# A mixture-of-experts step on one Trainium2 core: expert steps of two kinds alternate, and the weights of an expert are acknowledged in two parts

## The reference, cut to what matters

```python
score = jax.nn.sigmoid(jnp.dot(h, p['w_router']))
_, idx = lax.top_k(score + p['router_bias'], TOP_K)          # TOP_K = 8, N_EXPERTS = 64
g = jnp.take_along_axis(score, idx, axis=-1)
g = ROUTE_SCALE * g / jnp.sum(g, axis=-1, keepdims=True)
# for every block of tokens of one expert e, with their gates gb:
a = jax.nn.silu(xb @ w_gate_e[e]) * (xb @ w_up_e[e])
yb = a @ w_down_e[e]
acc = acc.at[tb].add(yb * gb[:, None])
shared = (jax.nn.silu(h @ p['w_gate_s']) * (h @ p['w_up_s'])) @ p['w_down_s']
```

## Time and profile before

| | us |
|---|---|
| median of three runs | 1594.47 |
| profiled execution, its own time | 1584.53 |
| profiled execution, span from first to last instruction | 1582.8 |
| TensorE busy | 1394.0 (88%) |
| VectorE busy | 650.3 (41%) |
| mean granted TensorE clock | 0.942 of full speed |

### The profile page before, as it was taken

The page is one execution under the profiler, slowest core; times in us unless marked ns, Lnnn a source line. Parts: engine busy times, 40 slices in busy tenths (PEclk is TensorE's granted clock), DMA queues, the critical chain, the costliest instruction groups (busy, mean ns, idle before and its releaser), DMA issues. The chain is left out here.

```text
span 1582.8 us, 30737 instructions
## 1 busy us (share of the span) xinstructions
PE 1394.0 (88%) x10030; PEld 741.6 (47%) x10031; DVE 650.3 (41%) x1888; ACT 387.5 (24%) x1026; POOL 245.3 (15%) x287
## 2 busy tenths in 40 slices
PE   6999799999989999788878877677999989999992
PEld 3445566666667776434543322222333333444441
DVE  1423266776676766244552222121222222332333
ACT  1102255444544444320100111111111111111110
POOL 1000200005263320010000111111121211122120
PEclk9999799999999999989799988888999999999996
DMA  8312499998989999760066999999999999975835
GB/s 306 58 27 63 153 297 291 326 319 288 304 276 300 320 305 317 254 239 27 21 249 233 368 374 380 374 369 375 365 371 355 370 368 364 350 234 182 273 80 196
DMA packets 159517, 424.12 MB, mean 268 GB/s; under 512 B 47825, under 2 KB 49906, under 8 KB 133234
## 3 DMA queue, kind: packets, MB, share of 16 engines
q1 hardware_dynamic: 142912, 381.59, 66.6%
q0 software_dynamic: 14400, 38.82, 10.0%
q10 hardware_dynamic: 2098, 2.35, 0.5%
HBM read 395.25 MB, written 41.06 MB: 276 GB/s over the span
## 5 line engine op out<-in xcount | busy, mean ns | idle before, releaser
L2475 PE MATMUL ps_gu<-ring,mixT 128*32 128x512 f32 (+2 forms) x1664 | 362.4, 633 | 68.5 <-SPq L2233 67.6
L2475 PEld LDWEIGHTS ps_gu<-ring,mixT 128*32 128x32 f32 (+2 forms) x1664 | 125.0, 140 | 301.7 <-issue 251.4
L2494 PE MATMUL ps_y<-w_dn,aT_e 128*32 128x512 f32 (+2 forms) x832 | 175.9, 598 | 4.5 <-DVE aT_e L2389 1.9
L1427 PE MATMUL ps_kT<-ident,ring 128*128 128x128 f32 x1024 | 144.5, 284 | 15.9 <-DVE ring L1093 8.5
L1427 PEld LDWEIGHTS ps_kT<-ident,ring 128*128 128x128 f32 x1024 | 116.3, 146 | 75.3 <-issue 48.6
L2387 DVE TENSOR_TENSOR act_in<-sil,ps_gu 128x256 f32<-128x256 f32 x48 | 20.2, 421 | 301.8 <-ACT sil L2307 301.8
L2259 POOL DMA_INDIRECT kT<-h_dram,idx x50 | 51.9, 1037 | 587.1 <-DVE idx L2348 587.1
L2307 ACT ACTIVATE sil<-ps_gu 128x256 f32<-128x256 f32 x48 | 18.4, 383 | 408.1 <-PE ps_gu L2475 408.1
L1093 DVE COPY ring<-ps_kT 128x512 f32<-128x512 f32 x128 | 87.8, 686 | 39.4 <-PE ps_kT L1427 38.4
L2263 POOL DMA_INDIRECT sums_dram<-qT,sidx x48 | 76.5, 1593 | 147.9 <-DVE qT L2397 143.9
L2494 PEld LDWEIGHTS ps_y<-w_dn,aT_e 128*32 128x32 f32 (+2 forms) x832 | 55.4, 132 | 93.4 <-issue 85.7
(11 more groups left out here) (504 smaller groups left out, 1796.0 us busy)
## 6 DMA issues: line engine op xcount, KB each, us to landing
ring<-in_cache_k SPq DMA_DIRECT2D x256, 256.0 KB
ring<-in_cache_v SPq DMA_DIRECT2D x256, 256.0 KB, 4.6
ring<-in_w_gate_e SPq DMA_DIRECT2D x64, 1024.0 KB
ring<-in_w_up_e SPq DMA_DIRECT2D x64, 1024.0 KB
w_dn<-in_w_down_e SPq DMA_DIRECT2D x64, 1024.0 KB
w_in<-in_w_in SPq DMA_DIRECT2D x8, 1028.0 KB, 16.3
sums_dram<-w_dn SPq DMA_DIRECT2D x1, 4608.0 KB, 19.6
ring<-in_w_out SPq DMA_DIRECT2D x1, 4096.0 KB, 13.0
```

What stands on the lines that cost most here:

```text
L1427: last = pe.transpose(ps_kT[:, j % 2, e * PAGE:(e + 1) * PAGE], k_places[n % RING][:, e * DA + j * P:e * DA + (j + 1) * P], m.ident[:, :])
L2475: last = pe.matmul(ps_gu[at, :].rearrange("p (g n) -> p g n", g=2), xgT[:, u, k, at], w_gu[:, place, :, k, :].rearrange("p s g n -> p (s g ...
L2494: last = pe.matmul(ps_y[at, n, :], aT[:, j, at], w_dn[:, place, j, n * 512:(n + 1) * 512].rearrange("p s n -> p (s n)"), start=(j == 0), s ...
```

## The change

The steps get a new order. With S2 steps of class two and S4 of class four (rounded up to even), the first A = min(S2, S4) - 2 steps of each kind alternate: a step of class two at each even place, one of class four at each odd place. Then come the other steps of class four, then the other steps of class two, then those of class three, as three loops on TensorE (`n_mix`, `n_four`, `n_two`) instead of two. The loads follow that order: before the two experts of a class-two step comes the expert of the class-four step of the same pair, if that step begins a new expert. In the alternating part a class-two step uses slots 0 and 1, and the experts of class four use slots 2 and 3 in turn; the slot of a load is now read from a table, `slot_tab`, as well. That needs more table work: the ranks, the step of each lane and the slots are computed on GpSimd in 51 instructions with 20 drains between them (`classes_done` to `slots_done`), one matmul (`begun_by_pair`) counts the class-four experts begun by each pair, and TensorE's `entries()` moves behind `shared(1, 0, range(KD), 0)`.

Only two experts are loaded in `mix_and_route`, the second when `gu_mm` is 2. Each slot has two semaphores, `gu_in` for gate and up and `dn_in` for down, and TensorE waits for `gu_ready` before gate and up and for `dn_ready` before down. In SyncE's loop, load `q` now first waits until gate and up of load `q - 1` have landed, and only then for the free slot, and issues gate and up; it issues down when down of `q - 1` has landed and the slot is free. Every fourth load it reads three tables of four entries.

```diff
-def load_gate_up(sp, a, m, e, s):
+def load_gate_up(sp, a, m, e, s, q):
 
     for i, name in enumerate(("w_gate_e", "w_up_e")):
-        sp.dma_start(m.w_gu[:, s, i, :, :], a[name][0, bass.ds(e, 1)].rearrange("e (p k) n -> p (e k) n", k=KD)).then_inc(m.w_in[s], 16)
...
+        sp.dma_start(m.w_gu[:, bass.ds(s, 1), i, :, :].rearrange("p s k n -> p (s k) n"),
+                     a[name][0, bass.ds(e, 1)].rearrange("e (p k) n -> p (e k) n", k=KD)).then_inc(m.gu_in[q % RING_W], 16)
...
-                first = registers(nc, mybir.EngineType.SP, m.load_tab, 0, RING_W, 0, NE - 1)
-                for s in range(RING_W - 1):
-                    load_gate_up(sp, a, m, first[s], s)
-                    if s == 2:
-                        sp.wait_ge(cleared, 16)
-                    load_down(sp, a, m, first[s], s)
-                s = RING_W - 1
-                sp.wait_ge(gu_mm, 2)
-                load_gate_up(sp, a, m, first[s], s)
-                load_down(sp, a, m, first[s], s)
+                experts_of = registers(nc, ENG.SP, m.load_tab, 0, 2, 0, NE - 1)
+                slots_of = registers(nc, ENG.SP, m.slot_tab, 0, 2, 0, RING_W - 1)
+                sp.wait_ge(cleared, 16)
+                for q in range(2):
+                    if q:
+                        sp.wait_ge(gu_mm, 2)
+                    load_gate_up(sp, a, m, experts_of[q], slots_of[q], q)
+                    load_down(sp, a, m, experts_of[q], slots_of[q], q)
...
+                pool.wait_ge(classes_done, 1)
+                tt(twos, of2, r2, ALU.mult)
+                tt(fours, of4, r4, ALU.mult)
+                tt(rank, of3, r3, ALU.mult)
+                ts(pool_i[:, 1, :], r3, 3.0, -5.0, ALU.mult, ALU.add)
+                pool.drain()
...
+                pool.drain()
+                pool.sem_inc(slots_done, 1)
...
+                dve.wait_ge(slots_done, 1)
+                ts(tmp2, order, -1.0, at_p, ALU.add, ALU.is_equal)
...
                 shared(0, 1, range(KD), 0)
+                begun_by_pair()
                 shared(0, 1, range(KD), 1).then_inc(gu_mm, 1)
+                shared(1, 0, range(KD), 0)
                 entries()
-                shared(1, 0, range(KD), 0)
                 shared(1, 0, range(KD), 1)
                 pe.wait_ge(tables_done, 1)
...
-                for e in range(RING_W, NE):
-                    s, r = e % RING_W, e // RING_W
-                    if s == 0:
-                        expert = registers(nc, ENG.SP, m.load_tab, e, RING_W, 0, NE - 1)
-                        free = registers(nc, ENG.SP, m.free_tab, e - RING_W, RING_W, 1, 2 * MAX_LOOPS)
-                    sp.wait_ge(gu_mm, free[s])
-                    load_gate_up(sp, a, m, expert[s], s)
-                    if e > RING_W:
-                        sp.wait_ge(w_in[s - 1], 48 * (r + 1) if s else 48 * r)
-                        sp.sem_inc(w_ready, 1)
-                    sp.wait_ge(dn_mm, free[s] * 2)
-                    load_down(sp, a, m, expert[s], s)
...
+                def gate_up_landed(q):
+                    sp.wait_ge(gu_in[q % RING_W], 32 * (q // RING_W + 1))
+                    sp.sem_inc(gu_ready, 1)
+
+                def down_landed(q):
+                    sp.wait_ge(dn_in[q % RING_W], 16 * (q // RING_W + 1))
+                    sp.sem_inc(dn_ready, 1)
+
+                gate_up_landed(0)
+                down_landed(0)
+                expert = slot = free = None
+                for q in range(2, NE):
+                    if q == 2 or q % RING_W == 0:
+                        n = 2 if q == 2 else RING_W
+                        expert = registers(nc, ENG.SP, m.load_tab, q, n, 0, NE - 1)
+                        slot = registers(nc, ENG.SP, m.slot_tab, q, n, 0, RING_W - 1)
+                        free = registers(nc, ENG.SP, m.free_tab, q, n, 1, 2 * MAX_LOOPS + 1)
+                    i = q - 2 if q < RING_W else q % RING_W
+                    gate_up_landed(q - 1)
+                    sp.wait_ge(gu_mm, free[i])
+                    load_gate_up(sp, a, m, expert[i], slot[i], q)
+                    down_landed(q - 1)
+                    sp.wait_ge(dn_mm, free[i] * 2)
+                    load_down(sp, a, m, expert[i], slot[i], q)
...
-                    pe.wait_ge(w_ready, needed)
+                    pe.wait_ge(gu_ready, needed)
...
                     pe.wait_ge(aT_done, step + 1)
+                    pe.wait_ge(dn_ready, needed)
...
-                step_of(0, 16, 0, 2, TWO[0], BEFORE)
-                step_of(1, 32, 1, 4, TWO[1], BEFORE + 3)
-                with pe.Fori(1, n_two) as i:
...
+                step_of(0, 16, 0, weights_of(0), TWO[0], BEFORE)
+                whole_step(1, 32, 1, BEFORE + 3)
+                with pe.Fori(1, n_mix) as i:
+                    step_of(i * 2, i * 16 + 16, 0, weights_of(i * 2), TWO[0])
+                    whole_step(i * 2 + 1, i * 16 + 32, 1)
+                with pe.Fori(n_mix, n_four) as i:
                     for u in range(2):
...
+                        whole_step(i * 2 + u, i * 16 + 16 * (u + 1), u)
+                with pe.Fori(n_four, n_two) as i:
+                    for u in range(2):
+                        step_of(i * 2 + u, i * 16 + 16 * (u + 1), u, weights_of(i * 2 + u), TWO[u])
+                with pe.Fori(n_two, n_loops, 3) as i:
                     for v in range(6):
...
+                        step_of(i * 2 + v, i * 16 + 16 * (v // 2 + v % 2 + 1), v % 2, weights_of(i * 2 + v), THREE[v % 3])
```

More of the change, by code:

```diff
@@ L1771, in mix_and_route @@
         iota_done, tables_done, x_again, cleared = sem("iota_done"), sem("tables_done"), sem("x_again"), sem("cleared")
+        const_done, classes_done, keys_done, begun_mm, ranks_done, bits_done, steps_done, slots_done = (
+            sem(x) for x in ("const_r", "classes_done", "keys_done", "begun_mm", "ranks_done", "bits_done", "steps_done", "slots_done"))
+        (count, n_big, in2, r2, of2, in3, r3, of3, of4, r4, blocks, cum, pair, at4, hit, key) = (cnt[:, i, :] for i in range(16))
+        tmp, ord4, end4, end3, end2 = (biased[:, i, :] for i in range(5))
+        end, lanes4, order, first, tmp2, ord3, prev4 = in2, in3, count, n_big, cum, rest[:, 0, :], rest[:, 1, :]
+        N2, S2, N3, S3, S4, A, S24, O3, B3, begun, of_rank = (n_f[:, i:i + 1] for i in range(11))
+        n_of, half_less, odd, is_odd, step_a, step_b, step_c = (by_step[:, i, :] for i in range(7))
+        lane_of = lane_f[:, 1, :]
+        slot_row, load_row, free_row = (pool_rows[:, i, :] for i in range(3))
         with nc.Block(no_gpsimd_drain=True) as block:
@@ L1822, in _ @@
+                tt(free, free, fours, ALU.add)
+                pool.drain()
+                ts(load_row, slot_row, float(NE), None, ALU.mult)
+                tt(free_row, free, rank, ALU.add)
+                pool.drain()
+                tt(load_row, load_row, exp_row[:, :], ALU.add)
+                pool.drain()
+                pool.sem_inc(slots_done, 1)
             @block.scalar
@@ L1922, in _ @@
                 dve.tensor_reduce(gsum[:, 0, :], gate[:, :, :], AX.X, ALU.add)
-                (count, n_big, in2, r2, of2, in3, r3, of3, of4, r4, b4, end, order, first, tmp, tmp2) = (cnt[:, i, :] for i in range(16))
                 stt = dve.scalar_tensor_tensor
                 ts = dve.tensor_scalar
-                N2, N3, W2, W3, B3, B4, O3, O4 = (n_f[:, i:i + 1] for i in range(8))
                 run = lambda out, x: dve.tensor_tensor_scan(out, m.ones[:, 0:NE], x, 0.0, ALU.mult, ALU.add)
+                at_p = blk_no[:, 0:1]
                 dve.wait_ge(rank_mm, 1)
@@ L1990, in _ @@
-                dve.tensor_reduce(n_f[:, 8:9], end, AX.X, ALU.max)
+                ts(A, S2, S4, -2.0, ALU.min, ALU.add)
+                tt(S24, S2, S4, ALU.add)
+                dve.tensor_reduce(begun, hit, AX.X, ALU.add)
+                dve.tensor_reduce(of_rank, end3, AX.X, ALU.add)
+                dve.drain()
+                dve.sem_inc(classes_done, 1)
+                ts(key, pair, A, float(P - 1), ALU.is_ge, ALU.mult)
+                ts(ord4, at4, A, 2.0, ALU.min, ALU.mult)
+                ts(B3, S24, float(QUAD), None, ALU.mult)
@@ L1991, in _ @@
+                tt(order, r2, ps[:, 3, TAB - 2 * NE:TAB - NE], ALU.add)
+                dve.drain()
+                tt(first, end, lanes4, ALU.subtract)
+                tt(order, order, of2, ALU.mult)
+                dve.wait_ge(steps_done, 1)
                 for i in range(TAB // P):
-                    ts(hits[:, i, 1, :], end, blk_no[:, i:i + 1], None, ALU.is_gt)
+                    ts(hits[:, i, 1, :], end, lane_of[:, i:i + 1], None, ALU.is_gt)
                 dve.drain()
+                tt(order, order, ord3, ALU.add)
@@ L1999, in _ @@
+                stt(order, order, float(RING_W), slot_row, ALU.mult, ALU.add)
                 tt(m.pos[:, :, :], ps[:, 3, 0:TT * NE].rearrange("p (t e) -> p t e", t=TT), tmp.unsqueeze(1).to_broadcast((P, TT, NE)), ALU.add)
+                dve.drain()
```

(5 more changed lines are left out.)

264 lines of the change are left out of this document (187 added, 77 removed).

## The result

The changed kernel takes 1606.67 us in the median of its runs (1598.8 to 1617.04), the kernel before took 1590.72 beside it (1581.69 to 1595.63): ratio 1.0131, 95% interval 1.0084 to 1.0178. It is slower by 13 to 28 us. The forecast was 1599, range 1570 to 1628. Ratios leave out the few executions in which the chip ran in a slower state, medians don't, so differences between kernels are taken from the ratios. The profiled execution took 1600.07 us, its span is 1598.1, 15.3 longer than before.

What follows compares the result with a forecast made beforehand. Loads were taken to pace classes two and three, TensorE class four. Pairing, reordering and the table stage gave -22 us, SyncE's waits +27: +5 against the span, forecast 1599 us on the median, range 1570 to 1628.

Steps and rivals of the forecast that it cites:

- What bounds the kernel, and the pairing: Expert stage: TensorE-bound class-four steps lend DMA time to load-bound class-two steps; last output 22 us earlier before wait losses.
- The rival that pairing gives nothing: Pairs: two-load intervals take 30 us like the others, as slots 0 and 1 lack a second buffer; 1615, chance 0.05.
- The three-load intervals: Six intervals between pairs that need three loads: 30.0 us each by the DMA price.
- The two-load intervals: Four intervals between pairs that need two loads: 26 us each, bounds 23.3 to 27.6, set by release of slots 0 and 1.
- The last pair to class three: After the pairs: next load held 50.5 us, 4 for register reads, then six loads in 61.6 us before class three.
- Class three: Last chapter of steps: five groups of 41.1 us and one of 37.9, plus 10 us loss from late issues.
- The order of SyncE's waits: SyncE's load loop: waiting for the previous landing before issuing gate and up loses 0.5 us a load, together 27 us.
- paid loads: Rival: every load waits for the slowest of 16 engines, 1.2 us each; 1636, counted from 0.7 on; chance 0.15.
- The full queue: Rival: gathers and scatters fill the DMA holes, loss at most 0.2 us a load; 1572 to 1583; chance 0.30.
- The table stage: Table work before the first expert step: ends 7 us later, bounds 2 to 14, with TensorE stalling 6.
- the table is late: Rival: some GpSimd table operations each cost 0.25 us more and TensorE stands 13 us more; 1612; chance 0.08.
- the main case: The forecast's own case: loss of 0.25 to 0.7 us a load, 1585 to 1612; chance 0.42.

Runs made afterwards that it cites:

- experiment 1: Changed kernel, but gate and up of a load issued before waiting for the previous landing (the early issue), except four loads: 1579.45 us, ratio 0.9956.
- Experiment 3: Kernel before with only the acknowledgement split (gate/up and down apart), release first and landing waited for after the issue: 1583.96 us, ratio 0.9978.
- experiment 4: experiment 1 with 8 alternating pairs in place of 12: 1590.06 us, ratio 1.0001.
- experiment 2: Kernel before, old order of steps, with the split semaphores and the changed kernel's order of waits: 1605.98 us, ratio 1.0093.
- experiment 5: Changed kernel with the table work it put on GpSimd done on VectorE: 1602.0 us, ratio 1.0061.
- experiment 6: Changed kernel with the changes of experiment 1 and experiment 5 together: 1569.7 us, ratio 0.989.
- experiment 9: experiment 8 with the table work on VectorE as well: 1563.51 us, ratio 0.9834.
- experiment 8: experiment 1 with class-four loads 8, 13, 21, 26 issued ahead of class-two loads, and 36 and 37 ahead of 33: 1572.96 us, ratio 0.9898.

## Why it came out so, step by step

**What bounds the kernel, and the pairing.** Right in the mechanism, 5 us too high in size. The forecast had the pairing and the new order bring 29 us between the first step and the end (-22 with 7 us of table stage taken off). With the early issue, experiment 1 needs 670.2 us from the first step to the last, the kernel before 694.7: -24.5. Experiment 3, the kernel before with the split alone, needs 689.9; if that is not spread, 4.8 of the 24.5 are the split's and 19.7 the order of steps. The rival that pairing gives nothing falls with that and with experiment 4.

**The three-load intervals.** Forecast 30.0 by the DMA price and 31.5 with the loss; measured 32.1 with it and 29.65 without (experiment 1). The price was right.

**The two-load intervals.** Forecast 26, 27.2 with the loss; measured 28.6, and 27.3 in experiment 1. This term was 1.3 to 1.4 us too low in each of four. The bounds of 23.3 to 27.6 hold experiment 1. Two of the four (29.7 and 29.6) follow a step whose gate and up took 8.87 and 9.55 us in place of 7.1, which delays the release of slots 0 and 1; less that, all four are 27.1 to 28.2. The forecast had not counted the clock; how much of the 1.4 it is, no run shows.

**The last pair to class three.** Forecast 119.1, measured 116.4; but the picture behind it was wrong, and that the number is near is in part luck. There are no 50 us of quiet DMA while the four class-four steps run: they had a share of 0.89, since each of them begins its own expert and frees a slot. No run shows which other term makes up for it.

**Class three.** Forecast 43.1 for a group of three steps with the loss, measured 216.5 / 5 = 43.3; without the loss 208.3 / 5 = 41.7 (experiment 1) against 41.1.

**The order of SyncE's waits, the term that decided.** Forecast 27 us, 0.5 a load. Undoing it gives back 28 us (experiment 1), and adding it to the old order costs 18 (experiments 2 and 3), so its mechanism is shown from both sides. Its place was mis-sized: 13.8 us in the pairs where the profiles show 20, 10 in class three where they show 8 to 9. Per load that is 0.77 us for the 26 loads of the ten intervals, above the 0.7 from which the forecast counted paid loads, and 0.4 for the 20 of class three; that the total came out at 27 against 28 is partly luck. The sign named for it, a share of 0.95 in both, came out as 0.88 and 0.98 (0.92 and 1.00 in experiment 1). In class three a load costs 43.3 / 4 = 10.8 us against 10.27, so 0.55 more, of which experiment 1 (10.4) takes 0.4 away. In the interval from 917.11 to 950.52 three loads stand behind one another at 11.1 us each, 0.9 above the price: with the release already there, each still waits for the one before. The full queue (loss below 0.25) and the fully paid load (1.2) both fall. The rule of the Trainium skill, page "DMA: Bandwidth & Descriptors", section "Rules for kernel authors", to issue early and wait late, pointed the right way. The worst case of 2 us a load that the forecast set beside it was not reached: the 28 us are 0.54 for each of the 52 loads.

**The table stage.** Forecast 7, bounds 2 to 14. From VectorE's first copy of the counts to the first step it is 72.1 us (783.36 to 855.45) against 58.2 (786.99 to 845.23): 13.9, at the upper bound. This is the term of the sum that was mis-sized the most for its length. Of the 6.9 us too much, 4.7 lie ahead of `entries()` (32.2 us from that copy, where 27.5 had been forecast), mostly GpSimd's chain, 21.2 us against 17: operations with one or two scalar operands read from a column (`n_f`, `pool_f`) took 0.44 to 0.90 us on 128x64 and 128x120, and plain ones on 128x120 took 0.44, where all had been costed by the 0.25 of the earlier trace rows. The other 2.2 lie behind it, 2.1 of them the half clock of the 20 matmuls after a stall of 11 us, where 6 had been forecast. In the profiled execution the stage began 3.6 us earlier than before, which hides a part, so the first step is only 10.2 later; this start is spread (779.76 to 797.90 over all profiles), the way from the copy on is steadier: 72.1 to 75.4 us in the seven profiles with GpSimd's chain, 58.2 to 60.1 in the three without the new tables. With the work on VectorE 10 to 11 us of it come back by the times of experiments 5, 6 and 9; in the profiles the way is 62.8 us in experiments 6 and 9, and 66.1 in experiment 5, which gives back 6 to 9 only and still has the 20 matmuls at 3.92 us. The rival "the table is late" was thus half true beside the main case. The forecast named 4 us by which a rule of the Trainium skill, page "GPSIMD Engine Reference", section "Engine selection", would lengthen the chain, and 4.2 were measured, but this is luck. The section puts GpSimd at about half of VectorE's speed for operations with two inputs and near line rate for those with one. The trace agrees on the first: plain operations with two inputs on 128x64 start every 0.27 us on GpSimd and, in the kernel before, every 0.14 on VectorE; the 0.24 and 0.32 that the forecast compared are durations, of one with a single input and one with two. It does not agree on the second: the dearest were operations with one input and scalar operands (0.79 us with two of them on 128x64, where VectorE took 0.32), and they, not a factor of two on all, lengthened the chain.

**The sum.** Against the span the forecast was +5, measured +15.3: 6.9 from the table stage, less the 3.6 of the earlier start, and 7.9 in the steps (3.7 in the three-load intervals, 5.7 in the two-load ones, 1.2 in class three, -2.7 in between); that makes 16.2, and the rest is rounding, mostly of the +5, whose terms add up to 4.5. On the medians of the runs it was 16, by the ratio 21. The absolute time was nearer, 1599 against 1606.67, since the kernel before had a median of 1590.72 beside the changed one and not the 1594.47 that the forecast added to; the change itself was three to four times what was forecast, clearly slower where +5 could not be told from no change. Both terms that decide were in the sum; what it had too low were the table stage and the intervals of the pairs.

## What to carry to other kernels

Wait for a transfer's landing only where its data or its slot is wanted, and never ahead of an issue that could go out on a release alone: one wait on the wrong side of the issue cost 28 us here, more than the 24.5 that split and reordering brought. When work moves to another engine, cost its operations by form (plain, with scalar operands, on one column) and not by one row, and ask what the engine behind it does to its clock while it waits. Moving loads into a hole of the DMA share moves the hole behind them if the load after waits for a release, as in experiment 8.

## What was not expected of the hardware

A wait of TensorE can cost more than its length. Behind several waits for weights the granted clock was half: in this window of the changed kernel, right after 7.85 us of idle time,

```profile
950.50:953.50 3.00, 2.98 (x8) 1.10 (x10) 0.00 (x0) 0.00 (x0) 0.00 (x0) 0.50 0.05 19
```

gate and up took 8.87 us in place of 7.1. Of the class-two steps of the pairs from the third on, six in the changed kernel took 8.8 to 9.6 us, 11.8 us too much in all, and three in experiment 1, 6.3 us; the 5.5 between them lie on the release of slots 0 and 1, so they would be about a quarter of the 20 us in the pairs; this is argued, no run took them apart. A wait of 2.81 us ahead of the step at 1040.87 left the clock whole, one of 2.46 us at 980.25 halved it for a part; what decides between them stays open. Small operations of GpSimd with scalar operands took up to 0.90 us on 128x120, twice the 0.44 of a plain one on the same shape. And DMA engines can be busy without moving much: 0.64 to 0.67 of the time at 98 to 115 GB/s in the microsecond in which a new load began to flow.
